# Gated scan of a hybrid transformer: the decayed query made two units ahead, ScalarE's exponential issued before the turned key's copy, and the second direction's output copied by ScalarE and added by GpSimd

## The reference

```python
def step(s, inp):
    qc, kc, vc, gc = (t.astype(F32) for t in inp)
    g = jnp.cumsum(gc, axis=2)
    ...
    att = jnp.einsum('bhik,bhjk,bhijk->bhij', qc, kc, decay)
    o = jnp.einsum('bhij,bhjv->bhiv', att, vc) + jnp.einsum('bhik,bhkv->bhiv', qc * jnp.exp(g), s)
    g_last = g[:, :, -1:, :]
    s = s * jnp.exp(g_last[:, :, 0, :, None]) + jnp.einsum('bhjk,bhjv->bhkv', kc * jnp.exp(g_last - g), vc)
    return s, o
...
for d in range(2):
    f = (lambda t: t) if d == 0 else (lambda t: jnp.flip(t, axis=2))
    ...
    ol = ol + f(gla_chunk_scan(f(ql), f(kl), f(vl), f(lgl[d]), s_ctx))
```

## Time and profile before

| | us |
|---|---|
| median of 3 runs | 3348.18 |
| lowest and highest | 3346.95, 3349.56 |
| the profiled execution | 3345.91 |
| its span in the trace | 3344.1 |

### The profile page before, as it was taken

The page is one execution under the profiler, slowest core; times in us unless marked ns, Lnnn a source line. Parts: engine busy times, 40 slices in busy tenths (PEclk is TensorE's granted clock), DMA queues, the critical chain, the costliest instruction groups (busy, mean ns, idle before and its releaser), DMA issues. The chain is left out here.

```text
span 3344.1 us, 56727 instructions
## 1 busy us (share of the span) xinstructions
PE 3025.9 (90%) x20258; PEld 2608.7 (78%) x20258; DVE 2016.3 (60%) x2829; ACT 1353.7 (40%) x2244; POOL 1469.7 (44%) x1161
## 2 busy tenths in 40 slices
PE   4999988986969999999999769989998789999999
PEld 3889966665849999999998647777777577778777
DVE  8977057788366655655564346666664565555555
ACT  3011155545134444444343335545453255555433
POOL 1322135552215555554764122212111267767687
PEclk8999989998979999999999869999999999999999
DMA  4558220002302222237322200000002122233723
GB/s 194 201 194 284 92 85 2 2 2 91 135 36 80 86 85 95 86 100 270 116 86 79 78 10 6 6 6 5 6 14 89 70 73 95 94 100 115 290 88 126
DMA packets 111704, 306.97 MB, mean 92 GB/s; under 512 B 12944, under 2 KB 26256, under 8 KB 108176
## 3 DMA queue, kind: packets, MB, share of 16 engines
q1 hardware_dynamic: 92208, 263.92, 23.2%
q10 hardware_dynamic: 19296, 40.26, 3.4%
HBM read 230.41 MB, written 73.73 MB: 91 GB/s over the span
## 5 line engine op out<-in xcount | busy, mean ns | idle before, releaser
L1624 PE MATMUL ps<-x_hi,w_hi 128*128 128x512 f32 (+3 forms) x1848 | 561.8, 343 | 62.1 <-DVE x_lo L1892 41.4
L1624 PE MATMUL ps<-x_hi,w_lo 128*128 128x512 f32 (+3 forms) x1848 | 554.4, 339 | 0.0
L1624 PEld LDWEIGHTS ps<-x_hi,w_hi 128*128 128x128 f32 x1848 | 332.8, 191 | 108.6 <-issue 54.1
L1624 PEld LDWEIGHTS ps<-x_hi,w_lo 128*128 128x128 f32 x1848 | 334.1, 191 | 25.0
L2005 DVE TENSOR_TENSOR d_lo<-d_raw,d_hi 128x640 fp32r<-128x640 f32 (+1 forms) x154 | 207.9, 1358 | 212.0 <-ACT d_hi L1799 212.0
L1507 POOL TENSOR_TENSOR w_lo<-up_raw,w_hi 128x512 fp32r<-128x512 f32 x176 | 235.8, 1345 | 220.9 <-ACT w_hi L1714 220.8
L1624 PE MATMUL ps<-x_low,w_hi 128*128 128x512 f32 (+3 forms) x1056 | 326.8, 337 | 0.0
L1543 POOL TENSOR_TENSOR dw_lo<-dn_a,dw_hi 128x512 fp32r<-128x512 f32 x154 | 218.2, 1419 | 160.2 <-ACT dw_hi L1796 160.0
L1641 PE MATMUL ps<-d_hi,dw_hi 128*128 128x320 f32 (+1 forms) x924 | 266.0, 342 | 21.4 <-DVE d_lo L2005 7.2
L843 POOL TENSOR_TENSOR k_decayed<-decay,qk 128x256 f32<-128x256 f32 (+1 forms) x240 | 193.5, 835 | 192.8 <-ACT decay L1008 192.8
L1507 POOL TENSOR_TENSOR w_lo<-w_sum,w_hi 128x512 fp32r<-128x512 f32 x132 | 174.6, 1323 | 213.4 <-ACT w_hi L1714 213.2
(11 more groups left out here) (290 smaller groups left out, 7846.8 us busy)
## 6 DMA issues: line engine op xcount, KB each, us to landing
up_raw<-in_up SPq DMA_DIRECT2D x88, 512.0 KB, 4.1
adaw_ring<-in_adaw SPq DMA_DIRECT2D x80, 512.0 KB, 4.1
d_raw<-blocks SPq DMA_DIRECT2D x77, 320.0 KB, 2.9
d_raw<-blocks SPq DMA_DIRECT2D x77, 256.0 KB, 2.6
dn_a<-in_dn SPq DMA_DIRECT2D x16, 1024.0 KB, 7.0
blocks<-t SPq DMA_DIRECT2D x44, 320.0 KB, 4.4
blocks<-t SPq DMA_DIRECT2D x44, 256.0 KB, 4.0
vr<-vr_out ACTq DMA_DIRECT2D x80, 128.0 KB, 2.8
```

The lines of the kernel that those rows point to most:

```text
L1624: mm = pe.matmul(c.psf[:, place[pos] + at:place[pos] + at + m], a[:, k, :], b[:, k, at:at + m], start=(k == 0 and a is w_hi[ring] and b is ...
```

## The change

Three edits, all in `gla_scan`.

1. DVE makes `q_decayed` two units ahead: `query(s, u + 2)` stands where `query(s, u + 1)` stood.
2. ACT issues `fade` and the exponential of unit u + 2 ahead of the copy of the turned key of unit u; before, the copy came first.
3. In the steps that aren't fresh, DVE no longer adds the output. ACT copies it from PSUM to a new tile `o_second` (`late`, two buffers), and POOL adds that tile to `o`. POOL's addition for unit u - 1 is written behind its three multiplications for unit u.

```diff
+    late = c.at("o_second", 203, [P, 2, GDV])
+    late_added = c.sem("o_second_added")
...
         def _(pool):
+            pool.sem_inc(late_added, U + 2)
+
+            def add_output(s, u, chunk):
+
+                d, h = divmod(u, GH)
+                oc = o[:, bass.ds(chunk[d], 1), h * GDV:(h + 1) * GDV]
+                pool.wait_ge(o_added, s * U + (u + 2))
+                pool.tensor_tensor(oc, oc, late[:, u % 2, :].unsqueeze(1), ALU.add).then_inc(late_added, 1)
+
             def body(pool, s, chunk, nxt, prev, fresh, prev_fresh):
...
                             ALU.mult).then_inc(k_set, 1)
+                    if isinstance(s, int) and s == 2 and u == 1:
+                        pool.wait_ge(late_added, 2 * U + 2)
+                        pool.sem_inc(late_added, 4 * U)
+                    if u and not fresh:
+                        add_output(s, u - 1, chunk)
+                    elif not u and prev and not prev_fresh:
+                        add_output(s + (-1), U - 1, prev)
             steps(pool, body)
+            add_output(NT - 1, U - 1, (NT - 1, 2))
...
-            def keep_output(s, u, chunk):
+            def keep_output(s, u, chunk, fresh):
...
                 act.wait_ge(o_done, s * U + (u + 3))
...
+                else:
+                    act.wait_ge(late_added, s * U + (u + 1))
+                    act.activation(late[:, u % 2, :], c.psf[:, O_PS:O_PS + GDV], ACT.Copy).then_inc(o_added, 1)
...
                 for u in range(U):
-                    act.wait_ge(turned, s * U + (u + 3))
-                    act.wait_ge(ks_done, s * U + (u + 1))
-                    act.activation(kt[:, u % 2, :], c.psf[:, TURN_PS:TURN_PS + P], ACT.Copy
-                                   ).then_inc(kt_set, 1)
                     fading(s, u)
                     if u + 2 < U:
                         decay(s, u + 2)
                     elif nxt:
                         decay(s + 1, u + 2 - U)
-                    if u and fresh:
-                        keep_output(s, u - 1, chunk)
-                    elif not u and prev_fresh:
-                        keep_output(s + (-1), U - 1, prev)
+                    act.wait_ge(turned, s * U + (u + 3))
+                    act.wait_ge(ks_done, s * U + (u + 1))
+                    act.activation(kt[:, u % 2, :], c.psf[:, TURN_PS:TURN_PS + P], ACT.Copy
+                                   ).then_inc(kt_set, 1)
+                    if u:
+                        keep_output(s, u - 1, chunk, fresh)
+                    elif prev:
+                        keep_output(s + (-1), U - 1, prev, prev_fresh)
...
-            def update(s, u, chunk, fresh):
-                d, h = divmod(u, GH)
-                if not fresh:
-                    oc = o[:, bass.ds(chunk[d], 1), h * GDV:(h + 1) * GDV]
-                    dve.wait_ge(o_done, s * U + (u + 3))
-                    dve.wait_ge(o_added, s * U + 1)
-                    dve.tensor_tensor(oc, c.psf[:, O_PS:O_PS + GDV].unsqueeze(1), oc, ALU.add
-                                      ).then_inc(o_added, 1)
+            def update(s, u):
...
             query(0, 0, (0, 1))
+            query(0, 1, (0, 1))
...
                     attention(s, u)
-                    if u + 1 < U:
-                        query(s, u + 1, chunk)
+                    if u + 2 < U:
+                        query(s, u + 2, chunk)
                     elif nxt:
-                        query(s + 1, 0, nxt)
+                        query(s + 1, u + 2 - U, nxt)
```

More of the change, by code:

```diff
@@ L968, in fading @@
                                ).then_inc(fade_set, 1)
-            def keep_output(s, u, chunk):
+            def keep_output(s, u, chunk, fresh):
                 d, h = divmod(u, GH)
                 act.wait_ge(o_done, s * U + (u + 3))
-                act.activation(o[:, bass.ds(chunk[d], 1), h * GDV:(h + 1) * GDV],
-                               c.psf[:, O_PS:O_PS + GDV].unsqueeze(1), ACT.Copy).then_inc(o_added, 1)
+                if fresh:
+                    act.activation(o[:, bass.ds(chunk[d], 1), h * GDV:(h + 1) * GDV],
+                                   c.psf[:, O_PS:O_PS + GDV].unsqueeze(1), ACT.Copy).then_inc(o_added, 1)
+                else:
+                    act.wait_ge(late_added, s * U + (u + 1))
+                    act.activation(late[:, u % 2, :], c.psf[:, O_PS:O_PS + GDV], ACT.Copy).then_inc(o_added, 1)
             def gate_input(s, d, chunk):
@@ L1044, in _ @@
             steps(act, body)
+            keep_output(NT - 1, U - 1, (NT - 1, 2), False)
         @block.vector
@@ L1113, in body @@
                     attention(s, u)
-                    if u + 1 < U:
-                        query(s, u + 1, chunk)
+                    if u + 2 < U:
+                        query(s, u + 2, chunk)
                     elif nxt:
-                        query(s + 1, 0, nxt)
+                        query(s + 1, u + 2 - U, nxt)
                     if u:
-                        update(s, u - 1, chunk, fresh)
+                        update(s, u - 1)
                     elif prev:
-                        update(s + (-1), U - 1, prev, prev_fresh)
+                        update(s + (-1), U - 1)
                     if nxt and u in (3, 7):
@@ L1128, in _ @@
             steps(dve, body, unrolled=True)
-            update(NT - 1, U - 1, (NT - 1, 2), False)
+            update(NT - 1, U - 1)
 def gla_finish(c, block, o, y_hi, y_lo, gnorm_d, vr_d):
```

## The result

| | before | after |
|---|---|---|
| median, us | 3347.56 (4 runs) | 3526.88 (4 runs) |
| lowest and highest, us | 3346.6, 3349.56 | 3523.7, 3528.63 |
| ratio | 1 | 1.0529, 95% interval 1.0516 to 1.0543 |
| span of the profiled execution, us | 3344.1 | 3525.6 |

The change makes the kernel 5.3% slower. The forecast was 3498 us, the range 3440 to 3540.

A forecast was written before the change was run, and what follows sets the result against it. The prediction took the scan to be bound by PE's products, DVE's picks and DVE's query in a ring. From 3345.9 us it took 15 off for the earlier query, added 165 for POOL's addition: 3496, median 3498 us, range 3440 to 3540.

The forecast's parts named there:

- the ring of products, picks and query: Scan before the change: PE's products, DVE's five picks, DVE's query, then products again set the pace, 4.20 to 4.22 us per unit.
- Part 1: Query two units ahead and exponential first, in the 40 fresh units of the scan: a gain of 15 us.
- The lower bound of 0: Fresh steps: no gain if DVE's query starts together with POOL's multiplications and takes 0.8 us more per unit.
- Part 2, the ring: Steps not fresh: products, decay, transpose, output, ACT's copy, POOL's addition and multiplications, next products form a chain; 165 us lost.
- The term for the ring at full clock: Steps not fresh: POOL's addition makes a period of 7.1 to 7.5 us instead of 4.20.
- The clock: Steps not fresh: PE's idle stretches drop its clock to the lower level in most units, raising the period to 8.3 us.
- an ordinary unit: Unit of the steps not fresh, before the gate pairs' share is added: period 8.3 us, between 7.4 and 8.9.
- a gate pair: Two per step, between decay and transpose in the steps not fresh: 1 us each, 0.25 us per unit.
- The sum: Whole kernel: 3345.9 - 15 + 165 = 3496 us for the profiled execution, so a median of 3498 us, 4.5% slower.
- rival 1: Steps not fresh: the new chain through POOL's addition, but at full clock; 3447 to 3464 us, chance 0.24.
- the second: Steps not fresh: PE at the lower clock throughout, period 8.8 us, gate pairs 2 us each; 3537 us, chance 0.10 with anything above.
- The third: Steps not fresh: ACT's copy is done before POOL comes to its addition, so all 80 units gain 0.37; 3318 us, chance 0.04.

The follow-up runs named there:

- the first experiment: The changed kernel, but POOL's addition for unit u - 2, not u - 1, stands behind its multiplications for unit u: 3331.26 us, ratio 0.9951.

## Why the prediction was right

**What bounds the kernel now**: the ring of products, picks and query was right. With the query moved away and the exponential early, PE no longer waits for it, and the fresh steps fell from 4.22 to 4.03 us.

**Part 1**: 15 us were taken for 40 fresh units, 0.2 x 40 = 8 came. The lower bound of 0 had the right reason: the query and POOL's multiplications start together. In the changed kernel POOL's three multiplications take up to 3.3 us in the fresh steps, where they took 2.40; the wait added in the experiment brings the period from 4.03 to 3.86. A thing that this part left out is that its two edits are not additive: alone, the first costs 14 us. The prediction took them together, so nothing of its sum was touched.

The Trainium skill, "SBUF — State Buffer", section "Who interferes with whom", has it that a DVE instruction with two SBUF inputs and a GpSimd instruction that reads SBUF contend for a shared port pair. It fits: the experiment that keeps the two instructions apart shortens both.

**Part 2, the ring**: right in every link, and shown by moving one row of POOL's program by one unit. The term for the ring at full clock was 7.1 to 7.5 us; with idle products it measured 7.3, and 7.45 with the gate pairs.

**The clock**: right that it falls, and at 51.5 us the clock's share is shown by experiment. The size was a little low. For an ordinary unit the prediction took 8.3 and the trace has 8.51. It reckoned that in some units the clock would fall too late to matter. But only in the first turn of each of the two stretches do the decay matmuls still end 2.06 to 2.09 us behind the products' start, as at full clock; in the others it is 2.4 to 3.25. One turn of the changed kernel in stretches, the first two without a matmul:

```profile
519.47:521.47 2.00, 0.00 (x0) 0.00 (x0) 1.08 (x2) 0.14 (x2) 2.00 (x4) 0.89 0.00 0
521.47:522.30 0.83, 0.00 (x0) 0.03 (x1) 0.00 (x0) 0.00 (x0) 0.69 (x2) 1.00 0.00 0
522.30:524.30 2.00, 2.00 (x51) 1.71 (x52) 0.91 (x3) 0.00 (x0) 0.00 (x0) 0.75 0.00 0
524.30:526.30 2.00, 2.00 (x6) 1.45 (x6) 0.78 (x3) 1.19 (x2) 0.00 (x0) 0.50 0.00 0
```

The clock is back at full speed while PE stands still and at the lower level again in the matmuls behind, so the means of 0.66 and 0.70 shown above make it look better than PE's work found it. For a gate pair the prediction took 1 us each, and it is 11.0 - 8.5 = 2.5. This is the term that was mis-sized: a pair of 1.05 us at full clock takes 2.07 at the lower one, all of it in the chain, since the exponential's cover ends long before, and the output's matmuls behind it run at the lower level too (1.06 us each). At full clock, with idle products, a pair costs 0.7 us.

**The sum**: 38 x (9.03 - 4.20) = 184, less 8, is 176 us. The spans differ by 181.5 (3525.6 - 3344.1). The 5 us between are mostly in the same 38 turns: counted from start to start of POOL's multiplications (to units 10 to 17 and 50 to 79) they take 344.9 us where they took 157.7 before, 187.2 more, because they took 4.15 each before and not 4.20, and take 9.08 after. The 41 others take 7.2 less. Two sums of the prediction are slightly off, and neither bears on the forecast: rival 1's upper end comes to 3462 and not 3464, and DVE's work per step with the lengthened query to 33.4 us and not 33.6.

**The rivals**: the second (lower clock throughout, 3537 us) was nearer to the result than the forecast. The third, that POOL's wait is already met, was rightly put down to PE's order, and the first experiment made it true by shifting POOL's order instead: its 3318 us were 3331, since only 0.2 us per unit and not 0.37 were to be had.

## What to carry to other kernels

An engine that works two units ahead keeps its lead only while nothing in its program waits for a result of the present unit. Here one instruction of 0.72 us put one place too early in POOL's queue cost 5 us per unit. Before work is moved to an engine with time to spare, write down what stands behind it there and who waits for that; an engine's idle share says nothing on it.

Two edits that look independent should be tried apart and together. Moving a producer earlier makes it wait for its own inputs earlier, and what stands in front of these in another engine's program becomes part of the path.

Where a chain leaves PE idle for some 3 us in each turn, as this one does, reckon the chain with the matmul times at the lower clock, all of them, gate pairs and other side work included.

## What was not expected of the hardware

- With an idle stretch of 2.8 to 3.8 us in each turn of 8 to 11 us, the granted clock was 0.66 and 0.70 of full speed in the mean of two stretches of 40 us in the steps that aren't fresh. The 4.6 to 8.2 us of matmuls in between ran at full speed for at most a part of each turn. The Trainium skill, "TensorE: Matmul & The Clock Gate", section "What's actually happening", says the slow clock is the default and activity lifts it, and the run with idle products agrees: 1.00 with them.
- Matmuls that compute nothing made a program 51.5 us faster.
- An added wait of POOL for DVE shortened the fresh steps from 4.03 to 3.86 us per unit (medians 3 to 5 us lower, with overlapping intervals). The two instructions lengthen one another where they meet: without the wait the query takes 1336 ns in the mean and not 1160, POOL's 384 columns 1278 and not 1014.
